# Last expert's gate and up weights in two transfers, and the down weights before the last in eleven

## The reference, cut to what matters

```
for l in range(2):
    x = x + concat(diff_attention, sparse_attention, mla)(rms_norm(x) @ w_in[l]) @ w_out[l]
    h = rms_norm(x)
    # router: best of 4 groups, then best 2 of its 8 experts
    for e in range(32):
        a = silu(h_e @ w_gate[l, e]) * (h_e @ w_up[l, e])      # 1024 x 512, twice
        x[tokens of e] += gate * (a @ w_down[l, e])             # 512 x 1024
x = rms_norm(x)
```

## Time and profile before

| | us |
|---|---|
| median of three runs | 1180.03 |
| lowest, highest | 1179.57, 1180.07 |
| profiled execution, whole | 1179.75 |
| span in its trace, first to last instruction | 1177.9 |
| TensorE matmuls busy | 930.4 |
| TensorE waiting for gate and up weights (`ring` and `arena`) | 112.4 and 70.2 |

### The profile page before, as it was taken

How to read it: one execution, slowest core, us unless ns; L and a number is a source line. 1 busy time by engine, 2 the same in 40 slices (tenths; PEclk the granted TensorE clock), 3 DMA queues, 4 the chain that set the end, 5 groups by cost and what they waited for, 6 DMA issues and landing times.

```text
span 1177.9 us, 23246 instructions
## 1 busy us (share of the span) xinstructions
PE 930.4 (79%) x10294; PEld 579.7 (49%) x10299; DVE 334.4 (28%) x974; ACT 195.2 (17%) x527; POOL 19.0 (2%) x38
## 2 busy tenths in 40 slices
PE   9999999767666866775799999997676667658765
PEld 5876666434334433443468766564343434334432
DVE  3646552211111111111237465521211121012112
ACT  2234321001000100010112442210010001001101
POOL 1000000000000000000000001000000000000000
PEclk9999999989788878888999999998887889788888
DMA  7956499999999999999997257999999999999994
GB/s 307 401 236 264 202 369 425 434 428 428 425 436 428 427 426 433 426 427 428 385 402 299 82 201 292 373 430 427 430 426 433 426 430 430 429 427 427 428 431 193
DMA packets 34167, 446.16 MB, mean 379 GB/s; under 512 B 9616, under 2 KB 11024, under 8 KB 14224
## 3 DMA queue, kind: packets, MB, share of 16 engines
q1 hardware_dynamic: 33504, 444.54, 89.8%
q10 hardware_dynamic: 560, 0.09, 0.0%
HBM read 443.57 MB, written 1.05 MB: 377 GB/s over the span
## 4 chain that ended last, share of the span: by engine, by line
DMA 47%; PE 46%; another core or an unknown queue 2%; issue 2%; ACT 1%; DVE 1%; POOL 0%; SPq 0%; ACTq 0%; POOLq 0%; DVEq 0%
DMA xb<-in_w_down 17%; DMA arena<-in_gate_up 15%; PE pv L1742 11%; DMA ring<-in_w_down 11%; PE pj L1368 8%; PE tr L1767 5%; DMA ring<-in_gate_up 4%; PE pj L1374 2%; PE pj L1777 2%; PE pj L1480 2%; PE pj L1600 2%; PE tr L1729 1%; PE pj L1575 1%; PE pj L1609 1%
## 5 line engine op out<-in xcount | busy, mean ns | idle before, releaser
L1742 PE MATMUL pv<-ring,xT 128*32 128x256 f32 x3072 | 223.4, 450 | 113.4 <-DMA ring<-in_gate_up 112.4
L1742 PEld LDWEIGHTS pv<-ring,xT 128*32 128x32 f32 x3072 | 108.5, 125 | 217.3 <-DMA ring<-in_gate_up 112.2
L1214 DVE TENSOR_SCALAR arena<-arena 128x128 f32<-128x128 f32 x64 | 14.5, 227 | 674.9 <-ACT arena L799 674.6
L1742 PE MATMUL pv<-arena,xT 128*32 128x256 f32 x1024 | 91.0, 528 | 70.2 <-DMA arena<-in_gate_up 70.2
L635 ACT ACTIVATE arena<-pv 128x256 f32<-128x256 f32 x64 | 24.5, 383 | 520.1 <-PE pv L1742 520.1
L1368 PE MATMUL pj<-xT,ring 128*128 128x256 f32 x448 | 100.2, 381 | 0.0
L1742 PEld LDWEIGHTS pv<-arena,xT 128*32 128x32 f32 x1024 | 40.8, 146 | 119.4 <-DMA arena<-in_gate_up 76.5
L1767 PE MATMUL tr<-ring,arena 128*32 128x256 f32 x1360 | 81.8, 380 | 14.9 <-issue 10.1
L1368 PEld LDWEIGHTS pj<-xT,ring 128*128 128x128 f32 x448 | 84.1, 190 | 13.1 <-issue 1.1
L1777 PE MATMUL pj<-arena 32*128 32x256 f32 x512 | 72.9, 400 | 6.7 <-ACT arena L635 6.7
L1777 PE MATMUL lg<-arena 32*128 32x256 f32 x512 | 72.7, 400 | 0.0
(11 more groups left out here) (237 smaller groups left out, 856.5 us busy)
## 6 DMA issues: line engine op xcount, KB each, us to landing
ring<-in_gate_up SPq DMA_DIRECT2D x42, 4096.0 KB, 48.5
ring<-in_w_down SPq DMA_DIRECT2D x38, 2048.0 KB, 41.5
arena<-in_gate_up SPq DMA_DIRECT2D x16, 4096.0 KB, 44.6
xb<-in_w_down SPq DMA_DIRECT2D x18, 2048.0 KB, 41.1
ring<-in_w_in_chunks SPq DMA_DIRECT2D x10, 2048.0 KB, 22.7
ring<-in_gate_up SPq DMA_DIRECT2D x10, 2048.0 KB, 8.2
ring<-in_w_out_halves SPq DMA_DIRECT2D x4, 2048.0 KB, 33.1
ring<-in_w_down SPq DMA_DIRECT2D x6, 1024.0 KB, 10.0
```

What stands on the lines that cost most here:

```text
L1742: ins = mm(gu_ps[i * CAP:(i + 1) * CAP, :], xg[:, j, c:c + CAP], w, start=(j == 0), stop=(j == KD - 1), tile_position=(0, i * CAP), skip_g ...
```

## The change

Two edits, both in the last round of each layer.

1. Gate and up weights of expert 31 come in two transfers, steps j = 0 to 3 and steps 4 to 7, each with a semaphore of its own (`last_steps_in`). `gate_up` of expert 31 waits for the first before step 0 and for the second before step 4, and no more for `gu_full`.
2. Down weights of expert 30 come in eleven transfers: ten of 8 partitions each (0 to 79), and one of the other 48. All eleven count on the same semaphore as before, for whose full sum `down` of expert 30 waits as before.

```
+EIGHTS, BY_EIGHT = N_EXPERTS - 2, 10
-D_LOADS = {1: 2, 2: 2}
+D_LOADS = {1: 2, 2: 2, EIGHTS: BY_EIGHT + 1}
+LAST_STEPS = ((0, 4), (4, 8))
...
+                            steps_of = gu_v[l * N_EXPERTS + e]
+                            if e == N_EXPERTS - 1:
+                                for n, (a, b) in enumerate(LAST_STEPS):
+                                    sp.dma_start(gu_place[i][:, a:b], steps_of[:, a:b]).then_inc(last_steps_in[n], 16)
+                            else:
+                                sp.dma_start(gu_place[i], steps_of).then_inc(gu_full[i], 16)
...
+                            elif e == EIGHTS:
+                                for n in range(BY_EIGHT):
+                                    ps = slice(8 * n, 8 * n + 8)
+                                    sp.dma_start(d_place[i][ps], rows_of[ps]).then_inc(d_full[i], 16)
+                                sp.dma_start(d_place[i][8 * BY_EIGHT:], rows_of[8 * BY_EIGHT:]).then_inc(d_full[i], 16)
...
                     for j in range(KD):
+                        for n, (first, _) in enumerate(LAST_STEPS):
+                            if in_pieces and j == first:
+                                pe.wait_ge(last_steps_in[n], 16 * (l + 1))
...
-                        pe.wait_ge(gu_full[n % GU_PLACES], gu_loads(l, n))
+                        if n < N_EXPERTS - 1:
+                            pe.wait_ge(gu_full[n % GU_PLACES], gu_loads(l, n))
```

More of the change, by code:

```diff
@@ L160, in upto @@
     def upto(last):
-        return sum(GU_LOADS.get(n, 1) for n in range(last) if n % GU_PLACES == e % GU_PLACES)
+        return sum(GU_LOADS.get(n, 1) for n in range(last) if n < N_EXPERTS - 1 and n % GU_PLACES == e % GU_PLACES)
     return 16 * at(layer, upto(N_EXPERTS), upto(e + 1))
@@ L354, in trunk @@
         last_in = [sem(f"last_in{n}") for n in range(len(LAST_PIECES))]
+        last_steps_in = [sem(f"last_steps_in{n}") for n in range(len(LAST_STEPS))]
         gain_f_in = sem("gain_f_in")
@@ L555, in _ @@
                             sp.wait_ge(gu_used[i], at(l, GU_FILLS, gu_uses(e)))
-                            sp.dma_start(gu_place[i], gu_v[l * N_EXPERTS + e]).then_inc(gu_full[i], 16)
+                            steps_of = gu_v[l * N_EXPERTS + e]
[4 more added lines that the diff above has]
+                                sp.dma_start(gu_place[i], steps_of).then_inc(gu_full[i], 16)
                         elif kind == "d" and e >= SPLIT:
@@ L1733, in gather, with gate_up @@
                     return last
-                def gate_up(both, c, other_half=0, signal=False):
+                def gate_up(both, c, other_half=0, signal=False, in_pieces=False):
                     for j in range(KD):
+                        for n, (first, _) in enumerate(LAST_STEPS):
+                            if in_pieces and j == first:
+                                pe.wait_ge(last_steps_in[n], 16 * (l + 1))
                         if j == KD // 2 and other_half:
@@ L1822, in products @@
                         gate_up(gu_landed(m * BODY + e), i * CAP,
-                                at(r, WIDE, gather_use(q) + 1) if i == 0 else 0, m == 0 and e == 0).then_inc(gu_done, 1)
+                                at(r, WIDE, gather_use(q) + 1) if i == 0 else 0, m == 0 and e == 0,
+                                m * BODY + e == N_EXPERTS - 1).then_inc(gu_done, 1)
                     def turned(e):
```

## The result

| | before | after |
|---|---|---|
| median | 1179.8 us (4 runs) | 1212.65 us (4 runs, 1211.66 to 1212.93) |
| ratio, 95% interval | | 1.0281 (1.0264 to 1.0298) |
| span of the profiled execution | 1177.9 us | 1211.0 us |

The account below looks back on a forecast made before the run. The weights' transfers bound the stages, with TensorE waiting at both layer ends for gate and up 31. Gains of 3.5 + 4.6 = 8.1 us from 1180.03 gave 1172.0 us; own range 1170.8 to 1174.5, 8 in 10 from 1170.5 to 1182.0.

Parts of the forecast that it names:

- What bounds the kernel, and the ends of the layers: Expert stages run at their weights' pace; at layer ends TensorE waits 3.42 and 3.09 us for gate and up 31.
- The split, 8.1 us or 5.4 if only it works: Layer ends: half of `gate_up` moves into the wait, 3.5 and 4.6 us; 5.4 if down 30 limits, chance 0.15.
- the sum: Whole kernel: gains of 3.5 and 4.6 us at the two layer ends, 8.1 together, giving 1172.0 us.
- Down 30 in eleven transfers: Layer ends: no gain alone; moves rows to early engines, so the late half lands 3.1 us earlier, keeping the split's gain.
- 5 rows more and 5 less: Down 30: one half of the engines gets 5 more rows, the other 5 fewer, 3.1 us later and 3.1 earlier.
- 13 against 3: Down 30: rows per engine, 10 + 3 on one half and 3 on the other, instead of 8 on each.
- Rival 3: Down 30's small transfers: eight engines get in each other's way on few paths; slower, priced at 1185.5 us, chance 0.20.
- far end: Down 30: small transfers at two engines' pace, 2.46 us each, 24.6 for ten in place of 6.1; 1202 us.
- the stagger that would keep engines apart: Down 30's small transfers: engines a row or two apart work on different transfers and partly avoid each other; 1185.5 us.
- The last sentence of the prediction: Layer ends: a landing of gate and up 31 itself that moves would show the prediction wrong altogether; no size given.
- the rule against it: Trainium skill's DMA port swizzle: four neighbouring partitions share a 27.2 GB/s port, so eight reach two ports, 54 GB/s.
- SyncE, nothing: Issue queue: ten more issues at 0.43 us, 4.3 us, plus one for the split, covered by 15 us; costs nothing.

Follow-up runs that it names:

- the first timing: Kernel before plus only the split of gate and up 31: 1176.06 us, 0.9971; timed again with more rounds, 1176.09 us, 0.9974.
- the order of the sixteen: Changed kernel, down 30 as sixteen half-row transfers of 8 partitions 4 apart plus one of 128: lower partitions first 1195.53 us, upper first 1191.84 us.
- the shapes alone: Kernel before plus unread transfers after its output, each shape on idle engines: 7.8 us for 2 MB, 7.3 for 1 MB in a block of 64.

## Why the prediction was wrong

*What bounds the kernel, and the ends of the layers.* Right. The stages run at their weights' pace, and all of the loss lies at the two layer ends (17.8 and 15.3 us).

*The split, 8.1 us or 5.4 if only it works.* The mechanism was right in each part: first half in the wait, second half at full clock behind 1.57 us, down 30 then 1.2 us late. It measures 3.3 us in the first timing and 3.7 in the second. In its first profile the weights of expert 31 land 0.7 us later than before (572.78 against 572.09), and in the second layer `down` of expert 30 ran once at the lower clock; the sum had no room for either. Neither need be a cost of the split, by what follows. The two runs that add transfers only after the output hold two more profiles of the kernel before: there the same weights land at 573.05 and 573.02 us, 1 us later than in the one profile from which the sum was made. The clock scatters too: in one of them `gate_up` of the second layer took 3.82 us behind a wait of 3.41, where the sum had counted on 6.57 behind 3.13.

*Down 30 in eleven transfers, nothing by itself and 3.1 us of shift between the halves.* This is the step that failed. Its assumption on the engines held: the small transfers use 8 engines, always the same, and the early ones (the single landings and the order of the sixteen show it). What failed is "5 rows more and 5 less": it let a row cost 0.61 us on whatever engine carried it, to whatever partition. In a stream of 8 neighbours a row costs 2.04 us alone, and it slows the large transfer beside it. The 0.61 us are the path's as well as the engine's: the shapes alone fit a path for each engine in a transfer of all 128 partitions, 26.7 GB/s for each, and two engines to a path in a block of 64, which runs at half the rate. The rows for partitions 64 to 127 need their paths for the same time whoever carries them, so the balance of the halves could not be shifted by choosing engines. The balance of row counts, 13 against 3, on which the forecast leant, said nothing about time.

*Rival 3, slower, 0.20.* Its mechanism is what happened, as far as it goes, and its far end, 2.46 us for a transfer of 8 neighbours and 1202 us, was the nearest: measured are 66 GB/s, 2.0 us each. That it came near in time is in part luck, since it had no effect on the weights ahead in the queue and too high a price for the small transfers. I priced it at 1185.5 for the stagger that would keep engines apart, for which there was no row. Against the far end's 22.2 us the measured 33.1 hold 5.3 us more of landing, where the block of 48 and the large transfer beside it were slowed as well (how the 5.3 divide was not measured), and 5.6 us of clock. The last sentence of the prediction named the sign, a landing of gate and up 31 that moves, and it moved by 8.4 us (580.49 against 572.04). The weighing was wrong in a general way: the balance was argued from a guess, the rule against it had a number, and with no row for either I gave the guess nearly three times the chance.

*SyncE, nothing.* Right for its issues (0.30 us each instead of 0.43). The queue did stall further behind them (12.08 us for the next layer's first two transfers), without a part in the loss: the first matmul that reads them, at 607.00 instead of 589.19, is late by the same 17.8 us as the `down` of expert 31 before it (600.49 instead of 582.68).

## What to carry to other kernels

By these runs a transfer into the on-chip memory is at its full 427 GB/s when its 128 partitions give each DMA engine a path of its own. Cut large transfers along the row, as gate and up 31 here, and not into blocks of partitions: a block of 64 runs at half rate, 8 neighbours at a sixth, and the weights queued before it are held up too. Where a profile shows a DMA share near 1 beside a low rate, look at the partitions that are being written. And where a forecast needs an engine to take over another's work, ask which second resource that work holds.

## What the runs showed that was not expected

- Engines run ahead of each other in two groups of eight by partition half; at the end of a layer the first engine of the group for 64 to 127 was 4.5 us behind the last of the other. Why it lags stays open.
- Transfers of 8 neighbours hold up engines that write elsewhere: 154 to 197 GB/s in place of 279 together, 3.4 to 3.6 us for a row that takes 1.21.
- Eight of 8 partitions take SyncE 2.64 us to issue when they are neighbours and 5.34 when they are 4 apart.
- 8 partitions 4 apart, in the half that their engines serve anyway, run beside a large transfer at the full 426 GB/s.
